# Sparse attention: two engines copy the shares of a group's sums side by side, and GpSimd adds them once per tile

## The chip, the cores and the metric

The kernel runs on 1 core of one Trainium2 chip. The metric is the device time of one execution in microseconds (us); a lower time is better. Engines are called by the names of the profile: PE (TensorE), PEld (its weight load), DVE (VectorE), ACT (ScalarE), POOL (GpSimd), SP (SyncE, which issues most transfers).

## What is computed

One layer of a hybrid encoder for 1024 prompt tokens and 32 sample tokens (D_MODEL 1024), in float32: RMSNorm, one input projection, three branches (a gated short convolution, sliding-window attention, sparse attention), each projected and weighted by a sigmoid gate, an output projection, a gated MLP with a convolution, and a final RMSNorm. The change touches the sparse attention, which has 8 query heads in 2 groups of 4, each group with one key/value head of 64 channels:

```python
def sparse_attend(q, k, v, idx, valid):
    b, Q = q.shape[:2]
    G = DSA_HEADS // DSA_KV
    kg = jax.vmap(lambda kk, ii: kk[ii])(k, idx)
    vg = jax.vmap(lambda vv, ii: vv[ii])(v, idx)
    qg = q.reshape(b, Q, DSA_KV, G, HEAD_DIM)
    s = jnp.einsum('bqkgd,bqskd->bqkgs', qg, kg).astype(jnp.float32) * SCALE
    s = jnp.where(valid[:, :, None, None, :], s, NEG)
    p = jax.nn.softmax(s, axis=-1)
    o = jnp.einsum('bqkgs,bqskd->bqkgd', p.astype(v.dtype), vg)
    return o.reshape(b, Q, DSA_HEADS * HEAD_DIM)
```

The output o (attn below) is multiplied by w_dsa_o and weighted by the branch's gate. Which keys a query takes (the 256 with the best indexer scores) is applied as a mask on dense scores, which DVE finds by rounds of MAX8 and MATCH_REPLACE8.

## The kernel before

**High and low halves.** Each float32 factor of a product is held as a high half (a fast rounding to fp32r) and a low half (the value less the high half), and PE makes three products: high by high, high by low, low by high. ACT makes nearly all high halves; POOL makes the low halves of the weights and of the attention's output, DVE those of the probabilities.

**The order of the work.** All queues are written out by hand, one per engine, with semaphores between them. The sparse attention (711 to 943 us) goes over 33 "pairs" of heads: one pair for the sample tokens and, for each tile of 128 queries (order TILES: 0, 1, 3, 4, 5, 6, 7, 2), two groups of two halves, each half being two heads. A step y of PE (attend_sparse, L1613) is: scores of a later pair (qk, L1528), transposes of pair y's probabilities by chunks of 256 keys (pt, L1552), a few tiles of the gate projections that fill PE's gaps (fill_sparse, the number from a table of costs, L143), and the products with the values (pv, L1567), the last chunk of a pair one step late. ACT's step (L2134) copies the high halves of the transposed probabilities, makes the high halves of the gates' weights, exponentials and half of the normalisations. DVE's step (attend, L2808) masks scores and finds their maxima (L2749), inverts the sums (L2761) and normalises a pair's first head (L2764), makes low halves of probabilities (L2793), and in the larger tiles runs rounds of the key search (L2564). For tile 3 and 4 and smaller ones the inversion stands at the step's start; from tile 5 on (a pair's "ahead" is 1) it stands behind the first low half and `output` of DVE. POOL's step (L1208) makes low halves of the gates' weights (L1084) behind ACT's high halves.

**The sums of a group.** The values are held as [high, low] in the columns of one 128-wide weight, so a group's product leaves two shares in one PSUM bank (bank 7, 128 partitions by 512): the share of the high values in the group's own 64 partitions, that of the low values in the other 64. When a group's second half is through (pv_done), ACT copies the low values' share into attn_sum (`low_share`, L2091, semaphore o_part). DVE waits for that and adds the bank's other half to it (`output`, L2796 to L2806, semaphore o_sum). ACT copies the group's high half to attn_hi (`output`, L2098). After both groups of a tile POOL makes the tile's low half attn_lo (`output`, L1148 to L1154). PE's first value product of the next group writes the same bank and waits for o_sum (L1572 to L1575). At the end PE waits for all attn_lo (L1641) and starts the projection of attn (L1642).

In the profile, the high and low copies and all other ACT copies have the line of their helper, L1853.

Of the kernel before, what the change touches and what calls it, by code (L numbers as in the profile page):

```python
# [23 lines left out]
ALU = mybir.AluOpType  # L24
ACT = mybir.ActivationFunctionType
F32 = mybir.dt.float32
# [3 lines left out]
P = 128  # L30
# [223 lines left out]
def build(nc, ins, outs):  # L254
    with ExitStack() as ctx:
        def sem(name):
            return ctx.enter_context(nc.semaphore(name))
# [36 lines left out]
        O_HI = place("attn_hi", [P, NJ, TOK], F32R, 24)  # L294
        O_LO = place("attn_lo", [P, NJ, TOK], F32R, 30)
        O_SUM = place("attn_sum", [P, NJ, TOK], F32, 30)
        G_LO = place("h2_lo", [P, KT, TOK], F32R, 24)

        MASK = place("key_mask", [P, SEL_COLS], F32, 34)
# [183 lines left out]
        pt_done, pt_hi, pt_lo, pv_done = sem("pt_done"), sem("pt_hi"), sem("pt_lo"), sem("pv_done")  # L483
        v_hi, v_lo = sem("v_hi"), sem("v_lo")
        o_part, o_sum, o_hi, o_lo = sem("o_part"), sem("o_sum"), sem("o_hi"), sem("o_lo")
        xr_in = [sem(f"xr_in{k}") for k in range(NT // 2 + 1)]

        xr_t, xr_out = sem("xr_t"), sem("xr_out")
# [278 lines left out]
        def parts_before(pair):  # L767

            return pair["o"] if pair["window"] else pair["o"] - 1

        def groups_of(pair):
            return range(NKV) if pair["sample"] else [pair["g"]]
# [273 lines left out]
        def _(pool):  # L1046
# [90 lines left out]
            def late_gate(q):  # L1137
# [7 lines left out]
                if p == 0 and w > 0:  # L1145
                    split(0, (J_WG + w + 1) // 2, (J_WG + w + 1) % 2, WIN)

            def output(pair):  # L1148

                if pair["sample"] or pair["half"] == 1 and pair["g"] == NKV - 1:  # L1150
                    at = slice(pair["i"] * P, pair["i"] * P + (DEC if pair["sample"] else P))
                    pool.wait_ge(o_hi, pair["o"] + 1)
                    nc.gpsimd.tensor_tensor(O_LO[:, :, at], O_SUM[:, :, at], O_HI[:, :, at].bitcast(F32),
                                            ALU.subtract).then_inc(o_lo, 1)  # L1154
# [53 lines left out]
            for y, pair in enumerate(SPARSE):  # L1208
                for c in range(len(pair["chunks"])):
                    sparse_split(y, c)  # L1210
                if y > 1:
                    output(SPARSE[y - 2])
            for pair in SPARSE[-2:]:
                output(pair)
            sparse_split(len(SPARSE), 0)
            for n in range(J_BC + 2, J_WO + 1):
# [99 lines left out]
        def _(pe):  # L1316
# [250 lines left out]
            def pv(pair, c):  # L1567

                q, g = pair["q"] + c, pair["g"]
                pe.wait_ge(pt_hi, q + 1)  # L1570
                pe.wait_ge(pt_lo, q + 1)
                if c == 0 and pair["half"] == 0:  # L1572
                    before = pair["o"] - (1 if pair["sample"] or (pair["i"], g) == (0, 0) or not pair["window"] else 2)
                    if before >= 0:
                        pe.wait_ge(o_sum, before + 1)  # L1575
                blocks = len(pair["chunks"]) * (1 if pair["sample"] else 2)
                for at, b in enumerate(pair["chunks"][c]):
                    if pair["sample"]:
                        v, rows = (VC[:, :], P) if b == 0 else (VS[0:DEC, :], DEC)
                        for h in range(NKV):  # L1580
                            last = nc.tensor.matmul(PS[:, sums_bank(pair, h), 0:P], v, PT_S[0:rows, q % 2, h * P:(h + 1) * P],
                                                    start=b == 0, stop=b == 1)
                        continue
                    key = pair["first"] + b
                    end = b == pair["chunks"][-1][-1]
                    for p in (PT_HI, PT_LO):
                        last = nc.tensor.matmul(PS[:, sums_bank(pair, g),  # L1587
                                                   2 * P * pair["half"]:2 * P * (pair["half"] + 1)],
                                                V_PARTS[:, key, g * P:(g + 1) * P],
                                                p[:, q % 2, 2 * P * at:2 * P * (at + 1)],  # L1590
                                                start=b == 0 and p is PT_HI, stop=end and p is PT_LO)
                last.then_inc(pv_done, 1)
# [258 lines left out]
        def _(act):  # L1851
# [246 lines left out]
            def output(pair):  # L2098

                act.wait_ge(o_sum, pair["o"] + 1)  # L2100
                for g in groups_of(pair):
                    last = copy(attn_rows(O_HI, pair, g), attn_rows(O_SUM, pair, g))
                last.then_inc(o_hi, 1)
# [30 lines left out]
            def attend_sparse(ps):  # L2134
# [7 lines left out]
                for y, pair in enumerate(ps):  # L2142
                    ahead, count = front(ps, y), len(pair["chunks"])
                    after = ps[y + 1] if y + 1 < len(ps) else None
                    for c in range(max(count, 4)):
# [8 lines left out]
                            exp(ahead, c)  # L2154
                        if c == 2 and after and after["ahead"] == 1:
                            normalise(after, 1)
                    if y > 0 and ps[y - 1]["last"]:
                        output(ps[y - 1])
                low_share(ps[-1])
                output(ps[-1])  # L2160
                sparse_gates(len(ps), 0)
# [256 lines left out]
        def _(dve):  # L2418
# [377 lines left out]
            def output(pair):  # L2796

                if pair["sample"]:
                    dve.wait_ge(pv_done, pair["q"] + len(pair["chunks"]))
                    for g in range(NKV):  # L2800
                        last = V_.tensor_copy(attn_rows(O_SUM, pair, g), attn_bank(pair, g, g))
                else:
                    g, out = pair["g"], attn_rows(O_SUM, pair, pair["g"])
                    dve.wait_ge(o_part, parts_before(pair))
                    last = V_.tensor_tensor(out, attn_bank(pair, g, g), out, ALU.add)
                last.then_inc(o_sum, 1)  # L2806
# [471 lines left out]
```

## Time and profile before

| | us |
|---|---|
| median of 3 runs | 1815.02 |
| lowest, highest run | 1814.38, 1815.6 |
| span of the profiled execution | 1813.3 |
| busy in it: PE, DVE, ACT, POOL | 1755.0, 1274.2, 726.8, 588.5 |
| sparse attention within it | 711 to 943 |

The span goes from the first to the last instruction of the profiled execution, and is 1.7 us below the median of the runs. Busy times overlap. A row of the timeline gives start, length, engine, line, operation, output<-inputs, and in brackets how long the engine stood idle before it and on whom it waited. In the timeline ops that an engine overlaps can share some time at their ends.

### The profile page before, as it was taken

Reading aid. Unit: us, or ns where it says so; the run is one execution under the profiler, and the core shown is the slowest. Engines: PE = TensorE matmul, PEld = TensorE weight load, DVE = VectorE, ACT = ScalarE, POOL = GpSimd, SP = SyncE. Lnnn points to the kernel's source line nnn. Section 1 sums busy time; section 2 is a strip of 40 time slices with the busy share of each in tenths; the row PEclk is TensorE's granted clock in tenths of the full one; section 3 lists DMA queues with packets and bytes.
Section 4 is the critical chain, followed back from the end, with each engine's and each line's share of the span. In section 5 each row is a group of like instructions: output and inputs, shape, how many; then the busy total and the mean of one; then the engine's idle time right before and its main releaser. Section 6 shows DMA issues by size and latency. Waiting matters only on the chain.

```text
span 1813.3 us, 32206 instructions
## 1 busy us (share of the span) xinstructions
PE 1755.0 (97%) x12267; PEld 1703.2 (94%) x12267; DVE 1274.2 (70%) x2222; ACT 726.8 (40%) x1273; POOL 588.5 (32%) x477
## 2 busy tenths in 40 slices
PE   5999999999999999898899999999999999999998
PEld 4999999989999998787789999999999999999998
DVE  6257869878788876688957347776666666776765
ACT  4333112348811133877763335333333333422334
POOL 2112212246633333422232000555555545121030
PEclk7999999999999999999999999999999999999998
DMA  4111111110111112311122311222222222542212
GB/s 151 36 35 36 47 36 47 47 39 25 42 41 44 48 39 71 88 41 36 47 59 88 102 46 36 95 83 72 83 84 71 83 72 74 192 135 79 91 36 96
DMA packets 180436, 121.22 MB, mean 67 GB/s; under 512 B 9340, under 2 KB 165260, under 8 KB 180300
## 3 DMA queue, kind: packets, MB, share of 16 engines
q1 hardware_dynamic: 179324, 117.37, 21.5%
q0 software_dynamic: 976, 2.00, 0.4%
q8 instruction: 90, 1.47, 0.3%
q14 instruction: 46, 0.38, 0.1%
HBM read 101.45 MB, written 17.89 MB: 66 GB/s over the span
## 4 chain that ended last, share of the span: by engine, by line
PE 87%; DVE 7%; ACT 2%; issue 2%; DMA 1%; POOL 1%; SPq 0%; DVEq 0%; ACTq 0%; POOLq 0%
PE ps L1329 36%; PE ps L1692 22%; PE ps L1765 7%; PE ps L1751 6%; PE ps L1449 3%; PE ps L1341 3%; PE ps L1472 3%; PE ps L1587 2%; PE ps L1547 2%; DVE probs L2749 1%; PE ps L1369 1%; DVE key_mask L2564 1%; DVE top L2564 1%; DMA x_rows<-in_x_prompt 0%; PE ps L1413 0%
## 5 line engine op out<-in xcount | busy, mean ns | idle before, releaser
L1075 POOL TENSOR_TENSOR w_lo<-w_raw,w_hi 128x1024 fp32r<-128x1024 f32 (+1 forms) x53 | 101.0, 1906 | 347.8 <-ACT w_hi L1853 347.8
L1329 PE MATMUL ps<-h_hi,w_hi 128*128 128x352 f32 (+1 forms) x912 | 199.5, 327 | 0.0
L1329 PE MATMUL ps<-h_hi,w_lo 128*128 128x352 f32 (+1 forms) x912 | 196.5, 323 | 0.0
L1329 PE MATMUL ps<-h_lo,w_hi 128*128 128x352 f32 (+1 forms) x912 | 196.2, 323 | 0.0
L2564 DVE MAX8 top<-key_mask 128x8 f32<-128x768 f32 (+5 forms) x192 | 170.4, 889 | 11.8 <-PE ps L1329 1.2
L2564 DVE MATCH_REPLACE8 key_mask<-top,key_mask 128x768 f32<-128x768 f32 (+5 forms) x192 | 167.7, 876 | 0.9 <-issue 0.9
L1329 PEld LDWEIGHTS ps<-h_hi,w_lo 128*128 128x128 f32 (+1 forms) x912 | 155.5, 186 | 0.5
L1329 PEld LDWEIGHTS ps<-h_hi,w_hi 128*128 128x128 f32 (+1 forms) x912 | 153.3, 187 | 2.6 <-issue 0.9
L1329 PEld LDWEIGHTS ps<-h_lo,w_hi 128*128 128x128 f32 (+1 forms) x912 | 154.2, 186 | 0.5
L1692 PE MATMUL ps<-mix_hi,quarter_hi 128*128 128x264 f32 x672 | 136.9, 285 | 0.5 <-ACT x_one L1853 0.5
L1692 PE MATMUL ps<-mix_hi,quarter_lo 128*128 128x264 f32 x672 | 136.4, 284 | 0.0
L1692 PE MATMUL ps<-mix_lo,quarter_hi 128*128 128x264 f32 x672 | 136.0, 284 | 0.0
L1853 ACT ACTIVATE w_hi<-w_raw 128x1024 fp32r<-128x1024 f32 (+3 forms) x90 | 72.9, 812 | 149.6 <-PE ps L1329 73.9
L2944 DVE TENSOR_TENSOR quarter_lo<-sum,quarter_hi 128x512 fp32r<-128x512 f32 x84 | 71.5, 870 | 57.1 <-ACT quarter_hi L1853 57.1
L1084 POOL TENSOR_TENSOR w_lo<-w_raw_in_lo,w_hi 128x512 fp32r<-128x512 f32 x44 | 57.4, 1307 | 152.5 <-ACT w_hi L1853 152.4
L1692 PEld LDWEIGHTS ps<-mix_hi,quarter_hi 128*128 128x128 f32 x672 | 104.3, 189 | 0.9 <-ACT x_one L1853 0.7
L1692 PEld LDWEIGHTS ps<-mix_lo,quarter_hi 128*128 128x128 f32 x672 | 104.2, 188 | 0.0
L1692 PEld LDWEIGHTS ps<-mix_hi,quarter_lo 128*128 128x128 f32 x672 | 103.9, 188 | 0.0
L1692 PE MATMUL ps<-h_hi,quarter_lo 128*128 128x264 f32 x504 | 103.1, 286 | 0.0
L1692 PE MATMUL ps<-h_hi,quarter_hi 128*128 128x264 f32 x504 | 102.5, 285 | 0.6 <-ACT z_one L1853 0.6
L1692 PE MATMUL ps<-h_lo,quarter_hi 128*128 128x264 f32 x504 | 102.8, 285 | 0.0
L2070 ACT ACTIVATE probs<-probs,softmax_stats 128x257 f32<-128x257 f32 (+11 forms) x132 | 81.9, 622 | 17.8 <-DVE softmax_stats L2777 9.1
(363 smaller groups left out, 4573.3 us busy)
## 6 DMA issues: line engine op xcount, KB each, us to landing
w_raw_in_lo<-in_w_in SPq DMA_DIRECT2D x56, 256.0 KB, 2.9
w_raw<-in_w_in SPq DMA_DIRECT2D x54, 256.0 KB, 3.0
ffn_tiles<-t SPq DMA_DIRECT2D x44, 264.0 KB, 2.4
w_raw<-in_w_gate SPq DMA_DIRECT2D x44, 256.0 KB, 3.1
w_raw<-in_w_up SPq DMA_DIRECT2D x44, 256.0 KB, 3.1
w_raw<-in_w_down SPq DMA_DIRECT2D x32, 192.0 KB, 2.7
w_raw_in_lo<-in_w_in SPq DMA_DIRECT2D x44, 128.0 KB, 2.2
ffn<-ffn_tiles SPq DMA_DIRECT2D x20, 264.0 KB, 4.4
```

The lines of the kernel that those rows point to most:

```text
L1075: nc.gpsimd.tensor_tensor(WLO[:, k, 0:tiles, :], raw[:, k, 0:tiles, :], WHI[:, k, 0:tiles, :].bitcast(F32), ALU.subtract).then_inc(lo_read ...
L1084: nc.gpsimd.tensor_tensor(WLO[:, k, tiles, :], WIN[:, k, tiles, :], WHI[:, k, tiles, :].bitcast(F32), ALU.subtract).then_inc(lo_half if pa ...
L1329: last = nc.tensor.matmul(PS[0:rows, NB * k + b, 0:e - a], w[:, k, t, 0:rows], x[:, t, a:e], start=m == 0 and w is WHI and x is hi, stop=m ...
L1341: last = nc.tensor.transpose(out, in_, IDENT[p0:p0 + r, p0:p0 + r])
L1449: last = nc.tensor.matmul(piece_bank(q), wt[:, w % 2, t, :], piece_at(x, t, p), start=t == 0 and wt is WHI and x is H_HI, stop=t == KT - 1 ...
L1692: last = nc.tensor.matmul(PS[:, 2 * pair + b, 0:QP], w[:, t * P:(t + 1) * P], x[:, tile + t, a:a + QP], start=first and t == 0 and w is WQ ...
L1751: last = nc.tensor.matmul(PS[:, NB * k + b, 0:PIECE], w[:, k, t, :], x[:, b * PIECE:(b + 1) * PIECE], start=t == 0 and w is WHI and x is F ...
L1765: last = nc.tensor.matmul(PS[:, 2 * pair + b, 0:QP], w[:, t * P:(t + 1) * P], x(t, b * QP, (b + 1) * QP), start=first and t == 0 and w is ...
L1853: return nc.scalar.activation(out, in_, ACT.Copy)
L2070: nc.scalar.activation(p, p, ACT.Exp, bias=stat[:, ub, 1, h:h + 1], accum_out=stat[:, ub, 2, h:h + 1]).then_inc(exp_done, 1)
L2564: step.mark(V_.max(top, s) if find else V_.match_replace(s, top, s, TAKEN))
L2944: V_.tensor_tensor(WQ_LO[q][:, :], src, WQ_HI[q][:, :].bitcast(F32), ALU.subtract).then_inc(q_lo_ready, 1)
```

## The change

It adds a buffer attn_share (at the place of attn_hi) and a semaphore o_share. For the 16 prompt groups of the sparse attention:

- DVE waits for pv_done in place of o_part, and copies its share from PSUM into attn_share; it no longer adds.
- PE's next group waits for both copies (o_part and o_share) in place of the sum.
- POOL adds attn_share to attn_sum, 128x512, once per tile, in the step after the tile's last pair, behind that step's first weight splits (`add_shares`). The low half attn_lo is made one step later than before (`y > 2` and `SPARSE[y - 3]`).
- ACT makes attn_hi once per tile, 128x512, in place of once per group, 64x512, and one step later.

The sample pair and the window attention stay as they are.

```diff
@@ -294,6 +294,7 @@
         O_HI = place("attn_hi", [P, NJ, TOK], F32R, 24)
         O_LO = place("attn_lo", [P, NJ, TOK], F32R, 30)
         O_SUM = place("attn_sum", [P, NJ, TOK], F32, 30)
+        O_SHARE = place("attn_share", [P, NJ, TOK], F32, 24)
         G_LO = place("h2_lo", [P, KT, TOK], F32R, 24)
 
         MASK = place("key_mask", [P, SEL_COLS], F32, 34)
@@ -483,6 +484,7 @@
         pt_done, pt_hi, pt_lo, pv_done = sem("pt_done"), sem("pt_hi"), sem("pt_lo"), sem("pv_done")
         v_hi, v_lo = sem("v_hi"), sem("v_lo")
         o_part, o_sum, o_hi, o_lo = sem("o_part"), sem("o_sum"), sem("o_hi"), sem("o_lo")
+        o_share = sem("o_share")
         xr_in = [sem(f"xr_in{k}") for k in range(NT // 2 + 1)]
 
         xr_t, xr_out = sem("xr_t"), sem("xr_out")
@@ -767,6 +769,14 @@
         def parts_before(pair):
 
             return pair["o"] if pair["window"] else pair["o"] - 1
+
+        def shares_before(pair):
+
+            return pair["o"] - SPARSE[1]["o"]
+
+        def ends_tile(pair):
+
+            return not pair["sample"] and pair["half"] == 1 and pair["g"] == NKV - 1
 
         def groups_of(pair):
             return range(NKV) if pair["sample"] else [pair["g"]]
@@ -1145,6 +1155,13 @@
                 if p == 0 and w > 0:
                     split(0, (J_WG + w + 1) // 2, (J_WG + w + 1) % 2, WIN)
 
+            def add_shares(pair):
+
+                at = slice(pair["i"] * P, (pair["i"] + 1) * P)
+                pool.wait_ge(o_part, parts_before(pair))
+                pool.wait_ge(o_share, shares_before(pair) + 1)
+                nc.gpsimd.tensor_tensor(O_SUM[:, :, at], O_SUM[:, :, at], O_SHARE[:, :, at], ALU.add).then_inc(o_sum, NKV)
+
             def output(pair):
 
                 if pair["sample"] or pair["half"] == 1 and pair["g"] == NKV - 1:
@@ -1208,9 +1225,12 @@
             for y, pair in enumerate(SPARSE):
                 for c in range(len(pair["chunks"])):
                     sparse_split(y, c)
-                if y > 1:
-                    output(SPARSE[y - 2])
-            for pair in SPARSE[-2:]:
+                    if c == 0 and y > 0 and ends_tile(SPARSE[y - 1]):
+                        add_shares(SPARSE[y - 1])
+                if y > 2:
+                    output(SPARSE[y - 3])
+            add_shares(SPARSE[-1])
+            for pair in SPARSE[-3:]:
                 output(pair)
             sparse_split(len(SPARSE), 0)
             for n in range(J_BC + 2, J_WO + 1):
@@ -1571,7 +1591,10 @@
                 pe.wait_ge(pt_lo, q + 1)
                 if c == 0 and pair["half"] == 0:
                     before = pair["o"] - (1 if pair["sample"] or (pair["i"], g) == (0, 0) or not pair["window"] else 2)
-                    if before >= 0:
+                    if not pair["window"] and not pair["sample"] and shares_before(pair) > 0:
+                        pe.wait_ge(o_part, parts_before(pair) - 1)
+                        pe.wait_ge(o_share, shares_before(pair))
+                    elif before >= 0:
                         pe.wait_ge(o_sum, before + 1)
                 blocks = len(pair["chunks"]) * (1 if pair["sample"] else 2)
                 for at, b in enumerate(pair["chunks"][c]):
@@ -2098,6 +2121,10 @@
             def output(pair):
 
                 act.wait_ge(o_sum, pair["o"] + 1)
+                if not pair["window"] and not pair["sample"]:
+                    at = slice(pair["i"] * P, (pair["i"] + 1) * P)
+                    copy(O_HI[:, :, at], O_SUM[:, :, at]).then_inc(o_hi, NKV)
+                    return
                 for g in groups_of(pair):
                     last = copy(attn_rows(O_HI, pair, g), attn_rows(O_SUM, pair, g))
                 last.then_inc(o_hi, 1)
@@ -2154,8 +2181,8 @@
                             exp(ahead, c)
                         if c == 2 and after and after["ahead"] == 1:
                             normalise(after, 1)
-                    if y > 0 and ps[y - 1]["last"]:
-                        output(ps[y - 1])
+                    if y > 1 and (ps[y - 2]["sample"] or ends_tile(ps[y - 2])):
+                        output(ps[y - 2])
                 low_share(ps[-1])
                 output(ps[-1])
                 sparse_gates(len(ps), 0)
@@ -2801,6 +2828,10 @@
                         last = V_.tensor_copy(attn_rows(O_SUM, pair, g), attn_bank(pair, g, g))
                 else:
                     g, out = pair["g"], attn_rows(O_SUM, pair, pair["g"])
+                    if not pair["window"]:
+                        dve.wait_ge(pv_done, pair["q"] + len(pair["chunks"]))
+                        V_.tensor_copy(attn_rows(O_SHARE, pair, g), attn_bank(pair, g, g)).then_inc(o_share, 1)
+                        return
                     dve.wait_ge(o_part, parts_before(pair))
                     last = V_.tensor_tensor(out, attn_bank(pair, g, g), out, ALU.add)
                 last.then_inc(o_sum, 1)
```

## Rows read from the trace of the kernel before

**Rows 1.** The page: the span, and the chain that ended last by engine.
```profile
span 1813.3 us, 32206 instructions
...
PE 87%; DVE 7%; ACT 2%; issue 2%; DMA 1%; POOL 1%; SPq 0%; DVEq 0%; ACTq 0%; POOLq 0%
```

**Rows 2.** Windows: stretch, length, busy us (instructions) per engine, clock, DMA share, GB/s.
```profile
711.00:943.00 232.00, 206.57 (x1458) 179.35 (x1458) 180.05 (x497) 169.90 (x351) 70.11 (x54) 0.99 0.23 58
```

**Rows 3.** Waits, 711 to 943 us: who <- for whom: us, times, longest.
```profile
PE ps L1587 <- DVE attn_sum L2805: 10.3, 11, 2.0
...
PE ps L1472 <- POOL w_lo L1075: 3.1, 1, 3.1
...
DVE attn_sum L2805 <- ACT attn_sum L1853: 8.4, 8, 2.2
```

**Rows 4.** Lines by form, 711 to 945 us (two last: whole run): busy, mean ns, idle.
```profile
L2805 DVE TENSOR_TENSOR attn_sum<-ps,attn_sum 64x512 f32<-64x512 f32 x16 | 11.0, 687 | 8.5 <-ACT attn_sum L1853 8.4
L1153 POOL TENSOR_TENSOR attn_lo<-attn_sum,attn_hi 128x512 fp32r<-128x512 f32 x8 | 10.3, 1291 | 2.2 <-ACT attn_hi L1853 2.2
L1853 ACT ACTIVATE attn_sum<-ps 64x512 f32<-64x512 f32 x16 | 9.5, 593 | 5.7 <-PE ps L1587 5.5
...
L3130 DVE COPY t<-ps 128x480 f32<-128x480 f32 x2 | 1.3, 658 | 0.7 <-PE ps L1675 0.7
...
L1235 POOL TENSOR_TENSOR sum<-w_raw 128x512 f32<-128x512 f32 x20 | 34.6, 1731 | 1.6 <-DMA w_raw<-in_w_up 1.6
```

**Rows 5.** Timeline of DVE and PE at three group ends (tiles 4, 2, 5).
```profile
798.15 0.68 DVE L2805 TENSOR_TENSOR attn_sum<-ps,attn_sum 64x512 f32<-64x512 f32 x1 [0.93 <-ACT attn_sum L1853]
...
798.98 0.36 PE L1587 MATMUL ps<-probs_t_hi,v_parts 128*128 128x256 f32 x1 [0.57 <-DVE attn_sum L2805]
...
934.93 0.36 PE L1587 MATMUL ps<-probs_t_hi,v_parts 128*128 128x256 f32 x1 [0.35 <-DVE attn_sum L2805]
...
848.31 0.36 PE L1587 MATMUL ps<-probs_t_hi,v_parts 128*128 128x256 f32 x1 [1.96 <-DVE attn_sum L2805]
```

**Rows 6.** Timeline: POOL and DVE side by side in tile 7, DVE in tile 6.
```profile
906.94 1.29 POOL L1084 TENSOR_TENSOR w_lo<-w_raw_in_lo,w_hi 128x512 fp32r<-128x512 f32 x1 [3.76 <-ACT w_hi L1853]
...
907.07 1.71 DVE L2764 TENSOR_SCALAR probs<-probs,softmax_stats 128x1024 f32<-128x1024 f32 x1
...
848.40 1.50 DVE L2764 TENSOR_SCALAR probs<-probs,softmax_stats 128x896 f32<-128x896 f32 x1
```

**Rows 7.** Timeline of DVE at the end of tile 6.
```profile
885.39 0.69 DVE L2805 TENSOR_TENSOR attn_sum<-ps,attn_sum 64x512 f32<-64x512 f32 x1
...
886.31 0.76 DVE L2764 TENSOR_SCALAR probs<-probs,softmax_stats 128x1024 f32<-128x1024 f32 x1
```

**Rows 8.** Timeline of DVE and PE after the end of tile 7.
```profile
924.13 0.42 DVE L2764 TENSOR_SCALAR probs<-probs,softmax_stats 128x384 f32<-128x384 f32 x1
...
926.24 0.63 PE L1341 MATMUL ps<-ident,probs 128*128 128x128 f32 x4 [0.27 <-issue]
```

**Rows 9.** Timeline of POOL, DVE and PE in tile 1.
```profile
751.19 2.54 POOL L1084 TENSOR_TENSOR w_lo<-w_raw_in_lo,w_hi 128x512 fp32r<-128x512 f32 x2
...
753.95 0.49 DVE L2764 TENSOR_SCALAR probs<-probs,softmax_stats 128x512 f32<-128x512 f32 x1
...
756.12 0.50 PE L1547 MATMUL ps<-k_hi,q_hi 64*128 64x512 f32 x2 [1.46 <-DVE softmax_stats L2749]
```

**Rows 10.** Timeline of POOL, DVE and PE in tile 2.
```profile
933.05 1.28 POOL L1084 TENSOR_TENSOR w_lo<-w_raw_in_lo,w_hi 128x512 fp32r<-128x512 f32 x1 [1.27 <-ACT w_hi L1853]
...
934.90 0.42 DVE L2764 TENSOR_SCALAR probs<-probs,softmax_stats 128x384 f32<-128x384 f32 x1
...
936.61 0.63 PE L1341 MATMUL ps<-ident,probs 128*128 128x128 f32 x4 [0.97 <-issue]
```

**Rows 11.** Timeline of POOL and PE at the end of the stretch.
```profile
943.22 1.27 POOL L1153 TENSOR_TENSOR attn_lo<-attn_sum,attn_hi 128x512 fp32r<-128x512 f32 x1 [2.21 <-ACT attn_hi L1853]
...
944.60 0.57 PE L1329 MATMUL ps<-attn_hi,w_hi 128*128 128x240 f32 x2 [0.70 <-issue]
```

## The prediction

> **What bounds the kernel now.** I read the page first: TensorE (PE) has 87% of the chain that ended last, VectorE (DVE) 7% [rows 1]. The edit lies in the sparse attention, 711 to 943 us. There the windows view shows PE busy 206.6 of 232 us, DVE 180.1, ScalarE (ACT) 169.9, GpSimd (POOL) 70.1 [rows 2]: PE leads, DVE is close, and POOL has room. The waits of that stretch give the target [rows 3]: PE waited 10.3 us in 11 places for DVE's add into attn_sum (the bank of sums is free only after it), and DVE waited 8.4 us in 8 places for ACT's copy of the other share. For the low halves of the gate weights, which POOL makes, PE waited once, 3.1 us, at the start of the stretch. So POOL has slack as a producer, and what can be won lies in the 11 places.
>
> There are 16 groups (8 tiles of two). Now pv_done, ACT copy, DVE add and PE are a chain. The forms give the prices [rows 4]: copy 593 ns, add 687 ns, POOL's low half 1291 ns.
>
> **The change, part by part.**
> (1) DVE's add becomes a copy from PSUM of 64x512. The nearest row is a PSUM copy of 128x480, 658 ns [rows 4]; scaled by columns that is about 0.69 us, the price of the add. DVE's busy time stays. Bounds: 0.59 us, as ACT's copy, to 0.70 us; I take 0.69, since the row is of the same engine and kind.
> (2) The copy no longer waits for ACT. PE resumes when both are done, so at best it gains the add. In tile 4's first group DVE stood idle 0.93 us for ACT's copy, added from 798.15, and PE idled 0.57 us until 798.98 [rows 5]. Now DVE copies beside ACT and the wait goes: **-0.57 us**. What is late next is PE's own gate work, which it still has to finish. At 934.93 PE idled 0.35 us [rows 5], but its next transposes idled 0.97 us more for the second half's probabilities [rows 10], and they depend on ACT's exp, which the edit does not move: 0. The 1.96 us before 848.31 [rows 5] is different: there the add follows at once on DVE's mask passes and low share, while ACT was done long before. A copy of the same length behind the same queue ends at the same time: 0. By the timeline this holds for seven of the 11 places (the adds at 773, 785, 830, 847, 867, 885 and 906 us), which hold 8.7 of the 10.3 us; of the other four, two are the rows above, and at 762 and 812 the wait shrinks by 0.2 to 0.3 us, but DVE's and ACT's own chain ends later there: 0. The bounds of this part are -10.3 us (all waits gone) and 0.
> (3) ACT makes 8 high halves instead of 16. A pass costs the same at 64 or 128 partitions (0.60 to 0.63 us), so 8 x 0.63 = 5 us of ACT work go. It stood at the end of a step, before a copy that waits for PE's transposes, so I take 0; bounds -5 and 0.
> (4) POOL gets 8 adds of 128x512, 10.3 us at the low half's 1291 ns [rows 4]. They stand in its queue ahead of the next weight splits, and wait for the last product of the tile. Each delays a split by up to 1.3 us plus the wait. Behind the split waits only PE's next gate job; from 762 us on each low half is ready 2 us or more before its use, so this costs 0.
> (5) What POOL's new ops do to DVE. At 906.94 a POOL subtract began, at 907.07 DVE's normalisation of 128x1024; it took 1.71 us and ended 0.55 us behind POOL's [rows 6]. The same op with POOL idle takes 0.76 [rows 7], so 0.95 us was lost. At 848.40 it is the same, with 1.50 us for 128x896 [rows 6]. The op that comes second stands until POOL's is through, and then ends after it by its length less 0.21 us. The Trainium skill says so too (SBUF — State Buffer, Who interferes with whom): DVE and GpSimd share a pair of ports by exclusive lock, and a tensor_scalar in a two-port mode blocks or is blocked for the whole instruction. It speaks against this change, and by that rule, too, the trace agrees (0.95 us).
>
> The new add starts about 0.06 us behind DVE's copy, and DVE's next op in the later tiles is exactly this normalisation, 0.2 us later. So the add comes first. Tile by tile:
> - End of tile 6: DVE's add ends 886.08, normalisation 886.31 to 887.07 [rows 7]. The new POOL add would run 886.14 to 887.43, the normalisation end at 887.43+0.55 = 887.98. DVE is the chain here: **+0.91 us**.
> - End of tile 7: the copy ends 923.8, POOL runs to 925.13, the normalisation of 924.13 (0.42 us) [rows 8] ends at 925.34 instead of 924.55. The second reciprocal follows the low share, ACT's scaling and PE's transposes at 926.24, which already wait 0.27 us [rows 8], follow that: **+0.5 us**.
> - End of tile 4: the same, but DVE waits for ACT soon after: **+0.2 us** (0 to 0.4).
> - End of tile 5: one of POOL's subtracts hits there already (848.40) and is only replaced by the add: 0. Tile 0: 0.9 us on DVE, absorbed before the next query-key product. Tiles 1 and 3: no normalisation behind the copy.
> (6) The low halves of the sums (POOL) move one step later. Tile 0's leaves 749.9 us and lands behind the two splits of 751.19 (2.54 us), which then start 0.4 us earlier: 753.34 to 754.63. DVE's normalisation of 753.95 (0.49 us) would end at 754.91, not 754.44; two mask passes later PE, idle 1.46 us before 756.12, waits for it [rows 9]: **+0.47 us**. Tile 7's lands behind the split of 933.05, 934.33 to 935.62, on the normalisation of 934.90 (0.42 us): it ends at 935.83, 0.5 us late, and PE's transposes at 936.61, idle 0.97 us, follow the second reciprocal behind it [rows 10]: **+0.5 us**. The others fall between normalisations.
> (7) The end of the stretch. PE's first merge product reads the last low half. Now: ACT's copy, DVE's add (0.69), ACT's high half, POOL's low half 943.22 to 944.49, PE at 944.60 after 0.70 us idle [rows 11]. After: DVE's copy is done 0.1 us behind ACT's, and the add of 0.69 us has become one of 1.29 us on POOL: 0.1 + 0.6 + 0.03 for the longer hop = **+0.73 us**, PE at 945.33. PE has no gap behind that place, so it goes to the end. Bounds: +0.6 (DVE's copy as short as ACT's) and +1.2 (POOL's add at 1731 ns, its dearest sum of 128x512 [rows 4]).
>
> The sum: -0.57 +0.91 +0.5 +0.2 +0.47 +0.5 +0.73 = +2.7 us. The profiled execution has a span of 1813.3 us [rows 1]; the median of three runs, 1815.02, is 1.7 us above, and I add the sum to the median: **1817.7 us**. Without the port terms of (5) and (6), the sum would be +0.2 us.
>
> **The rivals.**
> *Port lock everywhere* (slower). Place: all eight new adds, in front of DVE's normalisation. Price: 0.95 us each, the loss at 907.07 [rows 6], so 7.6 us, plus the moved low halves 0.97, the tail 0.73, less 0.57: +8.7, 1823.7 us. For it: PE's gaps in this stretch are nearly all waits for DVE or ACT, and once POOL is later, its splits can hit too. Against: only four adds have a normalisation right behind them, and one of these is hit already. Since 0.2% is 3.6 us, one more hit on the chain than I count decides it.
> *The waits go* (faster). If DVE, freed of its 8.4 us of waiting [rows 3], carries that to PE: -8.4 +0.73 = 1807.3 us. For it: PE waits on DVE in 11 places. Against: in seven of them DVE was late by its own work, and in most of the eight DVE stood idle next for ACT's probabilities anyway.
> *It frees nothing and hits nothing.* Share and sum come at the same time where PE waits, DVE's gaps swallow the lock, only tail and tile 4 count: +0.2, 1815.2 us. For it: DVE is idle 52 of 232 us [rows 2]. Against: the hits at 886 and 924 us lie where DVE or its followers have no gap.
>
> **How the numbers follow.** A measurement of this kernel can tell about 0.2%, 3.6 us, from no change. Chances: my sum 0.45, nothing 0.17, lock everywhere 0.28, waits go 0.10. The first two lie within 0.2%, so same 0.62, slower 0.28, faster 0.10. The range starts at 1812.5 (a third of the faster rival's gain) and ends at 1821.5 (two thirds of the slower one's step): two in ten are left out, half at each end. My sum's own range is 1815.2 to 1819.
>
> **What would show it.** Right: PE's waits for the sum in 711 to 943 us fall from 10.3 us by little, now to DVE's share copy of 0.69 us; four or more of DVE's normalisations last over 1 us, each over a POOL add; the gap before the first merge product grows from 0.70 to about 1.4 us; ACT's high halves are 8 fewer. Wrong: normalisations at their plain lengths while POOL adds (then the lock term falls), PE's wait for the share near 3 us or less with the stretch shorter (faster), or PE waiting for POOL's weight low halves (part 4).

## The result, and the profile after

The changed kernel took 1818.41 us (median of 9 runs, 1814.91 to 1819.54), the kernel before 1814.38 us beside it (9 runs, 1812.21 to 1815.6): a ratio of 1.0021, 95% interval 1.0012 to 1.0031, so 2 to 6 us slower. A second set of 11 runs gave 1817.19 us and 1.0022 (first experiment). The forecast was 1817.7 us, in a range of 1812.5 to 1821.5; the step was forecast as +2.7 us and measured, by the ratio, as +3.8.

The page of the changed kernel: span, busy time by engine, and the chain that ended last, to hold against [rows 1].

```profile
span 1817.1 us, 32237 instructions
...
PE 1754.3 (97%) x12267; PEld 1702.4 (94%) x12267; DVE 1279.9 (70%) x2222; ACT 721.5 (40%) x1265; POOL 599.4 (33%) x485
...
PE 86%; DVE 6%; ACT 3%; issue 2%; DMA 1%; POOL 1%; SPq 0%; DVEq 0%; ACTq 0%; POOLq 0%
```

The windows view of the sparse attention, the stretch of [rows 2] (PE, PEld, DVE, ACT, POOL, clock, DMA share, GB/s):

```profile
711.00:943.00 232.00, 203.86 (x1422) 176.53 (x1421) 183.55 (x494) 161.97 (x338) 77.02 (x59) 0.98 0.23 56
```

ACT has 8 us less to do in it, POOL 7 us more, and DVE, whose list of instructions did not get longer, is busy 183.6 us where it was 180.1 in [rows 2]. The waits of the same stretch, to hold against [rows 3]:

```profile
POOL attn_sum L1163 <- DVE attn_share L2833: 22.4, 6, 7.3
...
PE ps L1610 <- DVE attn_share L2833: 8.9, 8, 2.0
...
DVE attn_share L2833 <- PE ps L1610: 5.4, 4, 2.8
PE ps L1610 <- DVE probs_t_lo L2820: 5.1, 8, 1.0
...
PE ps L1492 <- POOL w_lo L1085: 3.1, 1, 3.1
```

DVE's 8.4 us of waiting for ACT's share are gone, and 5.4 us of waiting for the product itself stand in their place. PE's wait at the group ends fell from 10.3 us in 11 places to 8.9 in 8. It did not become a wait for POOL's weight halves: that row has its 3.1 us as before. The forms of 711 to 955 us, beside [rows 4]:

```profile
L2833 DVE COPY attn_share<-ps 64x512 f32<-64x512 f32 x16 | 11.0, 686 | 6.3 <-PE ps L1610 6.2
...
L1163 POOL TENSOR_TENSOR attn_sum<-attn_sum,attn_share 128x512 f32<-128x512 f32 x8 | 10.3, 1289 | 25.7 <-DVE attn_share L2833 23.4 <-ACT attn_sum L1876 2.3
...
L1170 POOL TENSOR_TENSOR attn_lo<-attn_sum,attn_hi 128x512 fp32r<-128x512 f32 x8 | 10.3, 1281 | 0.8 <-ACT attn_hi L1876 0.8
...
L2791 DVE TENSOR_SCALAR probs<-probs,softmax_stats 128x1024 f32<-128x1024 f32 x4 | 5.0, 1250 | 0.1
...
L1876 ACT ACTIVATE attn_hi<-attn_sum 128x512 fp32r<-128x512 f32 x8 | 5.0, 623 | 1.7 <-POOL attn_sum L1163 1.7
```

The new copy costs 686 ns (taken as 0.69), POOL's add 1289 ns (taken as 1291). The normalisation of 128x1024 is the row to look at: its plain length is 0.76 us [rows 7], its mean here 1.25. The timeline of DVE and POOL shows where: two rows of POOL's new adds, two of its moved low halves, and the DVE op that fell on each.

```profile
887.71 1.29 POOL L1163 TENSOR_TENSOR attn_sum<-attn_sum,attn_share 128x512 f32<-128x512 f32 x1 [4.75 <-DVE attn_share L2833]
...
887.77 1.78 DVE L2791 TENSOR_SCALAR probs<-probs,softmax_stats 128x1024 f32<-128x1024 f32 x1
...
889.59 0.69 DVE L2820 TENSOR_TENSOR probs_t_lo<-ps,probs_t_hi 128x512 fp32r<-128x512 f32 x1
...
916.52 1.29 POOL L1170 TENSOR_TENSOR attn_lo<-attn_sum,attn_hi 128x512 fp32r<-128x512 f32 x1
...
916.71 1.32 DVE L2598 TENSOR_SCALAR key_mask<-key_mask 128x384 f32<-128x384 f32 x1
...
928.26 1.30 POOL L1163 TENSOR_TENSOR attn_sum<-attn_sum,attn_share 128x512 f32<-128x512 f32 x1 [2.55 <-DVE attn_share L2833]
...
928.46 1.32 DVE L2791 TENSOR_SCALAR probs<-probs,softmax_stats 128x384 f32<-128x384 f32 x1
...
939.12 1.27 POOL L1170 TENSOR_TENSOR attn_lo<-attn_sum,attn_hi 128x512 fp32r<-128x512 f32 x1
...
939.72 0.88 DVE L2791 TENSOR_SCALAR probs<-probs,softmax_stats 128x384 f32<-128x384 f32 x1
```

Each of the four tensor_scalar ops of DVE began while POOL was at work and ended just behind it; their plain lengths are 0.76 [rows 7], 0.36 (in the kernel before, below), 0.42 [rows 8] and 0.42 [rows 10]. I call such an op a hit. What the hits of this kernel add:

| DVE op at | POOL op | plain, now | more, us |
|---|---|---|---|
| 740.75 | weight split | 0.35, 1.11 | 0.76 |
| 744.54 | add, tile 0 | 0.35, 1.39 | 1.04 |
| 748.27 | low half, tile 0, moved away | 0.86 before (at 749.22), 0.36 now | -0.50 |
| 753.11 | low half, tile 0 | 0.49, 1.10 | 0.61 |
| 814.92 | add, tile 4 | 0.62, 1.14 | 0.52 |
| 849.67 | add, tile 5 | 1.50 (already hit), 1.71 | 0.21 |
| 887.77 | add, tile 6 | 0.76, 1.78 | 1.02 |
| 916.71 | low half, tile 6 | 0.36, 1.32 | 0.96 |
| 928.46 | add, tile 7 | 0.42, 1.32 | 0.90 |
| 939.72 | low half, tile 7 | 0.42, 0.88 | 0.46 |

The end of the stretch, PE's first merge product, beside [rows 11]:

```profile
950.63 0.72 PE L1349 MATMUL ps<-attn_hi,w_hi 128*128 128x240 f32 x3 [1.58 <-issue]
```

PE idles 1.58 us there, 0.88 more than the 0.70 of [rows 11].

### The profile page after: what moved, and what is told of

It is laid out like the page before. It is cut to its first block, busy times and chain, and to the rows that moved or that the text cites. A ratio compares the mean times of both kernels' runs of the same rounds, so it can differ in the third digit from the quotient of the medians.

```text
span 1817.1 us, 32237 instructions
## 1 busy us (share of the span) xinstructions
PE 1754.3 (97%) x12267; PEld 1702.4 (94%) x12267; DVE 1279.9 (70%) x2222; ACT 721.5 (40%) x1265; POOL 599.4 (33%) x485
## 4 chain that ended last, share of the span: by engine, by line
PE 86%; DVE 6%; ACT 3%; issue 2%; DMA 1%; POOL 1%; SPq 0%; DVEq 0%; ACTq 0%; POOLq 0%
PE ps L1349 36%; PE ps L1715 22%; PE ps L1788 7%; PE ps L1774 6%; PE ps L1469 3%; PE ps L1361 3%; PE ps L1492 3%; PE ps L1610 2%; PE ps L1567 2%; DVE probs L2776 1%; PE ps L1389 1%; DVE key_mask L2591 1%; ACT probs L2093 1%; DVE top L2591 1%; DMA x_rows<-in_x_prompt 0%
```

## The experiments

The theory: POOL's new adds and its moved low halves stand just ahead of DVE ops that are then held up, and that, with the longer end, is the loss. The rivals: the loss comes from the share scheme itself (copies, one more hop, later high halves), or from POOL's time as such. Twelve kernels ran, in three groups on one chip each. The kernel before gave 1813.16 us (33 runs), 1813.59 (27) and 1813.66 (33) beside them; each kernel had 11 runs (the sixth 5), and an interval reaches 0.0009 to each side, 1.6 us (the sixth 0.0013). The ratios are those on record; the quotients of the medians differ from them by up to 0.0005, nearly 1 us.

| | kernel | median, us | ratio, 95% interval |
|---|---|---|---|
| 1 | the changed kernel | 1817.19 | 1.0022 [1.0013, 1.0031] |
| 2 | adds late | 1816.68 | 1.0019 [1.0010, 1.0028] |
| 3 | high and low halves one step earlier | 1816.83 | 1.0018 [1.0009, 1.0028] |
| 4 | before, and a POOL pass | 1815.08 | 1.0009 [1.0000, 1.0018] |
| 5 | last tile in the old form | 1817.75 | 1.0019 [1.0010, 1.0028] |
| 6 | DVE adds | 1821.73 | 1.0040 [1.0026, 1.0053] |
| 7 | adds late, low halves unmoved | 1814.07 | 0.9999 [0.9990, 1.0008] |
| 8 | 7, and the last tile in the old form | 1813.78 | 0.9997 [0.9988, 1.0006] |
| 9 | low halves alone unmoved | 1816.97 | 1.0016 [1.0007, 1.0025] |
| 10 | before, low halves moved | 1815.63 | 1.0012 [1.0003, 1.0021] |
| 11 | 7, and a POOL pass | 1815.63 | 1.0012 [1.0003, 1.0021] |
| 12 | 7 again | 1813.84 | 1.0000 [0.9991, 1.0009] |

**1. The changed kernel again**, as the measure for the first group. No edit.

> The changed kernel itself, unchanged, beside the runs below. Both theories expect +3 to +4.5 us against the kernel before (ratio 1.002). It sets the level from which the gain of the other kernels is read; DVE's copies of 0.69 us and five to seven of DVE's normalisations over 1 us, each over a POOL add or a moved low half, should come again at the same places.

It gave 1.0022, and the same hits at the same ops.

**2. POOL's adds late in the step**, behind all weight splits, so away from DVE's normalisation.

```diff
-                    if c == 0 and y > 0 and ends_tile(SPARSE[y - 1]):
-                        add_shares(SPARSE[y - 1])
+                if y > 0 and ends_tile(SPARSE[y - 1]):
+                    add_shares(SPARSE[y - 1])
                 if y > 2:
                     output(SPARSE[y - 3])
```

> POOL's add of the shares is moved from behind the first weight splits of the step to the step's end. Theory 1 (port lock: the add starts just ahead of DVE's normalisation): the hits behind the tile ends vanish, the normalisations at about 814, 888 and 928 us take their plain 0.62, 0.75 and 0.42 us, and 1.6 to 2.5 us come back against the changed kernel (so +1.5 to +2.5 against the kernel before). Theory 2 (the add costs because it holds up POOL's weight splits, or only the tail and the low halves count): no change against the changed kernel, within 0.7 us.

The adds' hits from tile 4 on went, in the timeline of this kernel:

```profile
887.16 0.76 DVE L2791 TENSOR_SCALAR probs<-probs,softmax_stats 128x1024 f32<-128x1024 f32 x1
...
914.16 1.32 DVE L2598 TENSOR_SCALAR key_mask<-key_mask 128x384 f32<-128x384 f32 x1
```

but those of the moved low halves stayed (754.46, 914.16, 936.68 us), and the time fell by 0.5 us only, within the error. So this run doesn't show that the adds' hits alone are the loss.

**3. High and low halves one step earlier**, as before the change, the adds early as in the change.

```diff
-                if y > 2:
-                    output(SPARSE[y - 3])
+                if y > 1:
+                    output(SPARSE[y - 2])
...
-                    if y > 1 and (ps[y - 2]["sample"] or ends_tile(ps[y - 2])):
-                        output(ps[y - 2])
+                    if y > 0 and (ps[y - 1]["sample"] or ends_tile(ps[y - 1])):
+                        output(ps[y - 1])
```

> ACT's high half and POOL's low half of a tile go back to the step where they were (one step earlier); the add stays. Theory 1 (the moved low halves hit DVE's normalisations in tiles 1 and 2 and the making of the last mask): DVE's ops at 753, 917 and 940 us take their plain 0.49, about 0.4 and 0.42 us, and 1.5 to 2 us come back against the changed kernel. Rival: the low halves' hits are absorbed, 0 to 0.3 us; or ACT, which now waits for POOL's add at the end of the step, gives 0.5 us or more of it away.

The low halves' hits went, the adds' stayed, and the time again fell by 0.4 us only. (Tile 0's low half is back on the normalisation at 748.77, 0.86 us, as in the kernel before.) In the medians each half of the theory alone gave next to nothing back; 7 tests both together.

**4. The kernel before, with one more POOL pass of 128x512** (1.04 us) in the place of the new adds, behind the last sum of tiles 1, 3, 4, 5, 6 and 7. It multiplies a finished low half by one; nothing else is changed.

```diff
+                    if c == 0 and y > 5 and y % 4 == 1:
+                        ...
+                        pool.wait_ge(o_sum, SPARSE[y - 1]["o"] + 1)
+                        ...
+                        nc.gpsimd.tensor_tensor(done, done.bitcast(F32),
+                                                ONES[:, :].unsqueeze(2).broadcast_to([P, NJ, P]), ALU.mult)
```

> The kernel before, with one POOL pass of 128x512 more at 6 of the 8 places where the changed kernel adds (behind the first splits of the step after tiles 1, 3, 4, 5, 6 and 7), on an earlier tile's low half, times one: no other engine waits for it. Theory 1 (port lock alone): normalisations over 1 us at about 849, 887 and 924 us and +1.4 to +2 us against the kernel before. Theory 2 (the cost is in the new waits and the tail): 0, within 0.5 us.

1.9 us more by the medians (interval 0 to 3.3). Its trace has the hits that the pass should make, on the path of a kernel without any of the share scheme:

```profile
888.88 1.44 DVE L2771 TENSOR_SCALAR probs<-probs,softmax_stats 128x1024 f32<-128x1024 f32 x1
...
928.37 1.10 DVE L2771 TENSOR_SCALAR probs<-probs,softmax_stats 128x384 f32<-128x384 f32 x1
```

**5. The last tile in the old form** (DVE adds, ACT makes the high half per group), the rest as changed, to price the end. Of the five places of the edit, DVE's is shown; PE's wait, ACT's high halves and POOL's last add go back in the same way.

```diff
...
-                    if not pair["window"]:
+                    if not pair["window"] and pair["i"] != TILES[-1]:
                         dve.wait_ge(pv_done, pair["q"] + len(pair["chunks"]))
...
```

> The changed kernel, but tile 2, the last, in the old form (DVE adds, ACT makes a high half per group, POOL adds nothing at the end). My sum: the tail's term goes, the time from the last value product to the first merge product falls from 4.35 to about 3.5 us, so 0.9 us against the changed kernel in that stretch. Rival (the tail is hidden behind ACT's last gate or the last weight split): no change there, 0 us.

PE's gap before the first merge product is back at its old length:

```profile
949.61 0.71 PE L1348 MATMUL ps<-attn_hi,w_hi 128*128 128x240 f32 x3 [0.69 <-issue]
```

From the last value product's end to the merge product it is 3.47 us here, 3.48 in the kernel before, 4.35 in the changed one: the end costs 0.87 us. In the medians, 0.87 us is too little to be seen (1817.75 us).

**6. DVE adds the shares itself**, once per tile, late in the step behind the tile; POOL has no add. The low halves stay moved.

```diff
...
+                        if y > 0 and ends_tile(ps[y - 1]):
+                            add_shares(ps[y - 1])
...
```

> The changed kernel, but DVE adds the shares itself, once per tile at the end of the step behind the tile, 128x512; POOL adds nothing. Theory 1 (port lock is the larger cost, the copy side by side gives about 0.6 us): all hits from POOL's adds vanish, DVE has 8 more passes of about 0.7 us (5.5 us of work), of which the ones in the tiles 4 to 7 (3 of them, where DVE is the chain) cost 2 us; against the kernel before +0.5 to +2.5. Theory 'the waits go': PE's waits for the share fall below 5 us and the time is under the kernel before by 1 us or more.

A miss: 8.1 us over the kernel before, where 0.5 to 2.5 was expected. I had taken DVE's idle time as cover. Against experiment 2, which has POOL's adds in this place, it is 1821.73 - 1813.59 = 8.1 against 3.5 us: 4.6 us more with eight DVE adds that take 6.0 us in all (seven of 0.69 or 0.70, and one of 1.17 at 933.76). So much of DVE's time in this stretch seems to be on the path, which would also be why a hit there counts. It isn't shown by this run alone: a normalisation of 1.33 us at 767.75 (plain 0.49) is in the 4.6 us too, and they weren't split further.

**7. Both: adds late and low halves unmoved** in POOL's queue. ACT's high halves stay one step later, as in the change.

```diff
-                    if c == 0 and y > 0 and ends_tile(SPARSE[y - 1]):
-                        add_shares(SPARSE[y - 1])
-                if y > 2:
-                    output(SPARSE[y - 3])
+                if y > 0 and ends_tile(SPARSE[y - 1]):
+                    add_shares(SPARSE[y - 1])
+                if y > 1:
+                    output(SPARSE[y - 2])
...
```

> The changed kernel with both POOL ops moved out of the way: the add at the end of the step behind the tile, the low half at the end of the next step and not the one after. Port lock theory: only tile 0's hit and the old ones at about 849 and 907 us stay; of the +3.8 us only the tail (0.9) and nearly nothing else remain, so +0.3 to +1.5 against the kernel before. If the cost has another source (queue order, ACT's later high half), +2.5 or more stays.

The whole loss is gone, within the error of 1.6 us: 1814.07 against 1813.59 us. The ops that were hit in the changed kernel, at plain length here (tile 0, tile 6, the mask):

```profile
753.29 0.49 DVE L2791 TENSOR_SCALAR probs<-probs,softmax_stats 128x512 f32<-128x512 f32 x1
...
885.53 0.75 DVE L2791 TENSOR_SCALAR probs<-probs,softmax_stats 128x1024 f32<-128x1024 f32 x1
...
913.53 0.36 DVE L2598 TENSOR_SCALAR key_mask<-key_mask 128x384 f32<-128x384 f32 x1
```

and PE's wait at the group ends (711 to 950 us) is

```profile
PE ps L1610 <- DVE attn_share L2833: 9.1, 8, 2.0
```

as large as in the changed kernel. So neither that wait nor the later high halves nor POOL's 10.3 us of adds are what made the change slow. The hits at 740.92 (1.12 us) and 744.71 (1.39 us) are still in this kernel, with a small new one at 769.64 (0.72 us, plain 0.49), and cost nothing that is seen.

**8. Experiment 7 with the last tile in the old form.**

> As the run before, and tile 2 in the old form. My terms leave the 0.57 us that the side-by-side copy gives in tile 4: -1 to +0.5 us against the kernel before. It is the version that could beat both; a gain of 1 us or more would mean that the side-by-side copies give more than my reading of the waits had.

1813.78 us, ratio 0.9997: the best of the changed forms, and a tie with the kernel before.

**9. Low halves alone unmoved**: as 7, but with the adds in their early place. (In 3, ACT's high halves had moved as well.)

```diff
-                if y > 2:
-                    output(SPARSE[y - 3])
+                if y > 1:
+                    output(SPARSE[y - 2])
...
```

> The changed kernel with GpSimd's low halves of the sums one step earlier again, so that they stand where the old kernel had them in the queue; ScalarE's high halves and GpSimd's adds stay as in the change. If the lock is what costs, and both kinds of op hit on the chain, this takes back the low halves' share: norms near 753 and 940 us and the mask op near 917 us at plain length, the hits of the adds (near 815, 888, 928 us) still there, median 1 to 2 us under the changed kernel (+2 to +3 over the kernel before). If the adds alone carry the loss, it stays at +3.5 to +4. If it was the low halves alone: +0 to +1.

1816.97 us. Between this and 7 and 12 lies only the place of the adds: +3.0 us (3.3 over the kernel before against 0.5 and 0.2).

**10. The kernel before, low halves moved one step later**, nothing else.

```diff
-                if y > 1:
-                    output(SPARSE[y - 2])
-            for pair in SPARSE[-2:]:
+                if y > 2:
+                    output(SPARSE[y - 3])
+            for pair in SPARSE[-3:]:
                 output(pair)
```

> The kernel before, with only GpSimd's low halves of the sums moved one step later; no share buffer, no adds. Lock theory: three hits come new (a normalisation near 753 us, the last mask op near 917 us, a normalisation near 935 us), the end of the stretch as before: +1 to +2 us. If what costs is the later high half or the new waits of the share scheme and not the place of the low halves: 0, within 0.5.

+2.0 us, with the three new hits:

```profile
752.30 0.90 DVE L2764 TENSOR_SCALAR probs<-probs,softmax_stats 128x512 f32<-128x512 f32 x1
...
914.31 1.34 DVE L2571 TENSOR_SCALAR key_mask<-key_mask 128x384 f32<-128x384 f32 x1
...
936.84 0.89 DVE L2764 TENSOR_SCALAR probs<-probs,softmax_stats 128x384 f32<-128x384 f32 x1
```

The mask op took 0.36 us in the kernel before (at 913.33). The three hits add 0.41, 0.98 and 0.47 us, 1.86 together, beside 2.0 measured (interval 0.5 to 3.8). A fourth, of a weight split at 739.95 (1.10 us, 0.38 in the kernel before), is the one that 7 has too without a loss.

**11. Experiment 7 with the POOL pass of experiment 4** in the place where the change had its adds.

> The kernel with late adds and low halves unmoved (it tied with the kernel before), and one more GpSimd pass of 128x512 in the place where the change had its adds, after tiles 1, 3, 4, 5, 6 and 7; its result is a tile's finished low half times one, needed by nobody new. Lock theory: the hits near 815, 888 and 928 us are back with it, +1.5 to +3 us over the kernel with late adds. If the gain of the late adds came from something else (the order of the high halves, the add's readiness), nothing comes back: within 0.7 of it.

+1.8 us over 12, and the hits are back, at the size that a pass of 1.04 us gives:

```profile
886.02 1.44 DVE L2798 TENSOR_SCALAR probs<-probs,softmax_stats 128x1024 f32<-128x1024 f32 x1
...
925.63 0.97 DVE L2798 TENSOR_SCALAR probs<-probs,softmax_stats 128x384 f32<-128x384 f32 x1
```

**12. Experiment 7 again**, on the chip of 9 to 11.

> The kernel with late adds and unmoved low halves once more, beside the others on the same chip. It should tie with the kernel before again, -1 to +1 us; if it comes out at +2 or more, its first result was luck and the lock theory has lost its main support.

1813.84 against 1813.66 us, a tie once more.

What hits add to DVE's ops is not yet what they add to the path. That can be read too, since DVE makes the same ops in the same order in every kernel: from the start of one such op to the start of the next, the distance is the same in all traces to some 0.03 us, except where a hit, a wait or the clock changes it. Around the mask op, in the kernel before and in the changed one:

```profile
913.33 0.36 DVE L2571 TENSOR_SCALAR key_mask<-key_mask 128x384 f32<-128x384 f32 x1
...
915.84 0.42 DVE L2764 TENSOR_SCALAR probs<-probs,softmax_stats 128x384 f32<-128x384 f32 x1
```

```profile
916.71 1.32 DVE L2598 TENSOR_SCALAR key_mask<-key_mask 128x384 f32<-128x384 f32 x1
...
920.18 0.42 DVE L2791 TENSOR_SCALAR probs<-probs,softmax_stats 128x384 f32<-128x384 f32 x1
```

The distance is 2.51 us, and 3.47 with the hit: 0.96 us more, the whole hit. The places, by their starts in the kernel before, with the full hits of the change (experiment 6, with DVE's own adds, is left out, and so are places where the clock stood at half in a trace; the last row ends at PE's first merge product and has the new end in both columns):

| from, to | not hit, us | hit, us | more | the op's own growth |
|---|---|---|---|---|
| 753.95, 765.48 (low half, tile 0) | 11.52 to 11.53 | 11.96 to 11.97 | 0.43 | 0.60 |
| 813.83, 822.10 (add, tile 4) | 8.27 to 8.28 | 8.41 to 8.43 | 0.15 | 0.52 |
| 848.40, 857.59 (add, tile 5) | 9.16 to 9.19 | 9.38 to 9.39 | 0.20 | 0.21 |
| 886.31, 896.38 (add, tile 6) | 10.06 to 10.07 | 11.07 to 11.09 | 1.02 | 1.02 |
| 913.33, 915.84 (low half, tile 6, on the mask op) | 2.51 to 2.52 | 3.47 to 3.49 | 0.96 | 0.96 |
| 924.13, 934.90 (add, tile 7) | 10.76 to 10.77 | 11.26 to 11.27 | 0.50 | 0.90 |
| 934.90, merge product (low half, tile 7) | 10.57 to 10.58 | 10.91 | 0.33 | 0.46 |

Together it is 3.6 us, and nothing of it is made up for later: from the op at 753.95 to the merge product it is 4.49 us more in experiment 1 than in 12, and 0.89 of them lie between 907.07 and 913.33, where in 1 the clock stood at half. The same distances give the pairs of kernels from 750 us on, in us (where the clock hides a place, the value of the same hit in another kernel is taken):

| pair of kernels | hits that differ | growth of the ops | on the path | medians differ by |
|---|---|---|---|---|
| 10 and before | 752, 914, 937 | 1.9 | 1.3, without 752, which can't be read | 2.0 |
| 2 and 7 | 754, 914, 937, less 7's own at 770 | 1.8 | 1.7 | 3.0 |
| 9 and 7 | 814, 848, 888, 928 | 2.7 | 1.9 | 2.8 |
| 11 and 12 | 814, 848, 886, 926 | 1.3 | 0.7 | 1.8 |
| 4 and before | 815, 850, 889, 928 | 1.6 | 0.8 | 1.9 |
| 1 and 7 | all seven from 750 us on, less 7's own | 4.5 | 3.6 | 3.6 |
| 1 and 2 | the adds' from 813 us on | 2.7 | 1.9 | 0.5 |
| 1 and 3 | the low halves', less 3's own in tile 0 | 1.5 | 1.0 | 0.4 |
| 1 and 9 | the low halves', less 9's own at 770 | 1.8 | 1.7 | 0.7 |

(The pairs 2 and 7, 9 and 7, 1 and 7, 1 and 9 are from two groups, each less its own kernel before.) Each difference of medians is uncertain by 1.6 to 2 us, and all nine lie within 1.4 us of the path's column, so single rows prove little. By the medians alone it looked as if the hits didn't add up: with one kind taken away, the time fell by half a microsecond, with both by 3.6. In the traces of 2, 3 and 9 the path is shorter by all that the missing hits had cost, so that looks like the error of the medians.

## Why the prediction was right, by its steps

The outcome (slower by about 0.2%, at the edge of what a measurement tells) and its cause, hits of POOL's ops on DVE's normalisations, were as forecast. "Without the port terms of (5) and (6), the sum would be +0.2 us": experiments 7 and 12 take out the port terms from 750 us on and measured +0.5 and +0.2.

- Part 1, the copy's price: 0.69 us forecast, 686 ns measured.
- Part 2, the wait that goes (-0.57 us): **this step failed.** PE's waits at group ends fell by 1.4 us, from 10.3 to 8.9; in seven of the places DVE was late by its own work, as read. The wait of 0.57 us in tile 4 went, but nothing came of it: the DVE normalisations on either side of it (796.01 and 805.53 in the kernel before) are 9.52 us apart in the kernel before and 9.53 in the changed one. Just ahead of them 0.14 us was gained (6.60 to 6.46 us from 789.41 on); that is all from 753.95 us on.
- Parts 3 and 4, ACT's eight high halves fewer and POOL's adds in the queue: 0 each, and 7 bears it out, with PE's wait for POOL's weight halves still one of 3.1 us.
- Part 5, forecast, and found on the path: tile 6 +0.91, 1.02; tile 7 +0.5, 0.50; tile 4 +0.2, 0.15; tile 5, "only replaced", 0, but 0.20 (the op went from 1.50 to 1.71 us, since the add began 0.05 us before it and not 0.27). Tile 0's 1.04 us was indeed absorbed: to the next normalisation it is 3.73 us, where it was 3.85.
- Part 6: the moved low halves of tiles 0 and 7, +0.47 and +0.5 forecast, cost the path 0.43 and 0.33. **Here a second step failed:** "The others fall between normalisations." Tile 6's low half did, but hit the last mask op instead, 0.36 to 1.32 us, all 0.96 us of it on the path. I had searched DVE's queue for normalisations, not for every op of the same kind. Nor did I see that tile 0's low half already hit a normalisation at its old place (749.22, 0.86 us) and frees it by leaving, a term that the forecast lacked. Experiment 3, which has that hit still, takes 0.69 us more than 1 from 742.26 to 753.95 (13.04 and 12.35 us). A first-tile split also hit at 740.75, as in 7, where no loss is seen.
- Part 7, the end: +0.73 forecast, 0.87 measured. The hop from DVE's copy to POOL's add is 0.17 us, not 0.06 (886.85 + 0.69 to 887.71).

By the path then: -0.14 + 1.02 + 0.50 + 0.15 + 0.20 + 0.43 + 0.33 + 0.96 + 0.87 = +4.3 us, against 3.8 measured with an interval of 2.2 to 5.6. The forecast's 2.7 took 0.4 us too much off for the waits, and lacked the mask op and tile 5. The port terms that it had were right in place, and most in size; that the missing terms came to no more than 1.2 us is luck, since DVE's other ops hadn't been looked through.

The range's upper end was said to be two thirds of the slower rival's step; two thirds of 8.7 give 1820.8 us, not 1821.5. The result lies below both.

Of the rivals, the lock everywhere (+8.7) took eight adds at 0.95 us; five adds hit, one of these hits was absorbed, and of the other four only tile 6's cost the path as much. The waits did not go: freeing DVE of 8.4 us of waiting brought PE 1.4 us fewer waits, and the path 0.14.

What stays open: whether the share scheme gives anything ahead of 750 us. From 753.95 us to the merge product experiment 12 is longer than the kernel before by 0.74 us, the end's 0.87 less 0.14; before that place the traces differ by more than a microsecond in either direction, and the medians can't tell it. Between 710 and 955 us TensorE's granted clock also stood at half (1.2 GHz) for 7 to 17 us, in pieces of 3.4 us or twice that, and in part at other places in each profile, so that the length of the whole stretch in one profile is no good measure.

## What to carry to other kernels

When work moves onto GpSimd, or only changes its place in GpSimd's queue, list every VectorE op of the tensor_scalar kind, from SBUF to SBUF, that can start while it runs, mask and helper ops too, and let each end behind GpSimd's op by its own length less 0.2 us. Then ask how much of that the path keeps: here between none and all of it. The free engine is not free: its place in the step decides, and the same adds a few microseconds later in the step, with the low halves left where they were, cost nothing that is seen. And where the waiting engine waits because another is late by its own work, taking a link out of the chain between them gave nothing here.

## What the runs showed of the hardware

- A DVE TENSOR_SCALAR that starts 0.05 to 0.6 us into a POOL TENSOR_TENSOR of 1.29 us ended 0.55 us behind it at 128x1024 (887.71 + 1.29 = 889.00, 889.55) and 0.22 us behind it at 128x384 (928.26 + 1.30 = 929.56, 929.78): its own length less about 0.2 us. The mask op, with a plain length of 0.36, also ended 0.22 us behind (916.52 + 1.29 = 917.81, 918.03).
- Unlike these, an op that reads PSUM, the low half at 889.59 (0.69 us, its usual length), was not lengthened while POOL's next split ran (from 888.97, 1.72 us). The Trainium skill (SBUF — State Buffer, Who interferes with whom) says both: an op in a two-port mode is shut out for the whole of GpSimd's instruction, one with at most one SBUF input and outside those modes isn't. The trace agrees.
- It works in the other direction too: in experiment 7 a POOL add that began inside a held DVE op took 1.68 us in place of 1.29.

```profile
847.64 1.48 DVE L2791 TENSOR_SCALAR probs<-probs,softmax_stats 128x896 f32<-128x896 f32 x1
...
848.59 1.68 POOL L1163 TENSOR_TENSOR attn_sum<-attn_sum,attn_share 128x512 f32<-128x512 f32 x1
```

- ACT's high half took 0.623 us for 128x512, and 0.624 for 64x512 in the kernel before: the partitions didn't count. The columns did, with 0.30 to 0.31 us for 64x128.
- A DVE copy from PSUM of 64x512 took what the add of a PSUM and an SBUF operand of that size had taken (686 and 687 ns).
